# Input projections of the even mixer block as three passes over rounded and remainder parts, in a two-layer diffusion backbone on one core

## What is computed

```python
def half_ffn(h, mod, j, w, g, b, alpha):
    y = swiglu(modulate(h, mod, j), *w)          # (silu(h @ gate) * (h @ up)) @ down
    return layer_norm(alpha * h + 0.5 * gate(mod, j) * y, g, b)
# even layer: h <- LN(a*h + g_1 * W_out[mixers(mod_1(h) @ W_in)])
# W_in columns: NA q, k, v (512 each), mLSTM xm, v, o (512 each), 8 + 8 gate columns
def even_mixer(zc, zl, rpb, conv_w, conv_b, wq, wk, i_bias, f_bias, gn_w):
    pc, pl = split_cols(zc, EV_SIZES), split_cols(zl, EV_SIZES)
    na_c = context_attention(heads(pc[0]), heads(pc[1]), heads(pc[2]))
    na_l = neighbourhood_attention(..., heads(pc[1]), heads(pc[2]), rpb)
    xs_c, o_c = mlstm_prepare(pc[3:], conv_w, conv_b, wq, wk, i_bias, f_bias)
    ...
    h_c, h_l = bidir_scan(mlstm_scan, xs_c, xs_l, ((), ()), init, 2)
```

## Time and profile before

| | us |
|---|---|
| median of 3 runs | 2009.19 (2009.07 to 2010.22) |
| span of the profiled execution | 2008.5 |
| TensorE busy | 1905.3 (95%) |
| VectorE busy | 1263.0 (63%) |
| ScalarE busy | 648.5 (32%) |
| GpSimd busy | 290.2 (14%) |

### The profile page before, as it was taken

One profiled execution on the slowest core, in us unless ns is written; L12 is line 12 of the kernel. 1 busy time (PEld: TensorE's weight loads), 2 busy tenths in 40 slices (PEclk: granted clock), 3 DMA queues, 4 the chain that ended last, 5 costly groups with the idle time before them and its releaser, 6 DMA issues.

```text
span 2008.5 us, 24119 instructions
## 1 busy us (share of the span) xinstructions
PE 1905.3 (95%) x9168; PEld 1512.3 (75%) x9168; DVE 1263.0 (63%) x2217; ACT 648.5 (32%) x1102; POOL 290.2 (14%) x313
## 2 busy tenths in 40 slices
PE   5999999999998789899999989999999899989997
PEld 5888878884554455788887878888778866879997
DVE  7677777664864573877769367673777444464454
ACT  2322242323334441422224233222433232434453
POOL 0000001160000003400001131000044435130002
PEclk7999999999997899899999989999999999989999
DMA  9354545431440001454543233544134644204543
GB/s 363 123 199 182 190 161 153 146 120 61 177 179 0 1 0 43 158 198 175 206 175 144 87 155 132 204 172 177 48 134 176 252 179 152 89 38 168 196 157 108
DMA packets 43958, 290.10 MB, mean 144 GB/s; under 512 B 13916, under 2 KB 19676, under 8 KB 27232
## 3 DMA queue, kind: packets, MB, share of 16 engines
q1 hardware_dynamic: 35488, 271.13, 36.8%
q10 hardware_dynamic: 8384, 17.83, 2.3%
HBM read 272.16 MB, written 16.78 MB: 144 GB/s over the span
## 4 chain that ended last, share of the span: by engine, by line
PE 83%; DVE 9%; DMA 4%; ACT 3%; issue 1%; POOL 0%; SPq 0%; ACTq 0%; POOLq 0%; DVEq 0%
PE bank L623 13%; PE bank L628 13%; PE bank L625 13%; PE bank L680 6%; PE bank L689 6%; PE bank L686 6%; PE bank L810 4%; PE bank L807 3%; PE bank L794 3%; PE bank L989 2%; DMA slot<-in_down_dram 2%; PE bank L747 2%; DMA R<-in_ada_dram 1%; PE bank L737 1%; PE bank L986 1%; PE bank L944 1%
## 5 line engine op out<-in xcount | busy, mean ns | idle before, releaser
L1720 DVE CUSTOM_DVE_ANT_0 L<-slot 128x1024 f32<-128x1024 f32 x272 | 337.6, 1241 | 86.1 <-DMA slot<-in_ada_dram 79.0
L1173 ACT ACTIVATE w_hi<-slot 128x1024 fp32r<-128x1024 f32 x176 | 186.3, 1061 | 572.4 <-PE bank L628 561.2
L1777 DVE TENSOR_TENSOR w_lo<-slot,w_hi 128x1024 fp32r<-128x1024 f32 x176 | 216.8, 1234 | 206.6 <-ACT w_hi L1173 200.4
L623 PE MATMUL bank<-m_hi,w_hi 128*128 128x512 f32 (+1 forms) x1344 | 296.6, 363 | 3.2 <-ACT w_hi L1173 3.2
L628 PE MATMUL bank<-m_hi,w_lo 128*128 128x512 f32 (+1 forms) x1344 | 296.1, 362 | 0.0
L625 PE MATMUL bank<-m_lo,w_hi 128*128 128x512 f32 (+1 forms) x1344 | 296.1, 362 | 0.0
L623 PEld LDWEIGHTS bank<-m_hi,w_hi 128*128 128x128 f32 x1344 | 232.3, 189 | 43.1 <-ACT w_hi L1173 4.0
L628 PEld LDWEIGHTS bank<-m_hi,w_lo 128*128 128x128 f32 x1344 | 232.6, 189 | 39.3
L625 PEld LDWEIGHTS bank<-m_lo,w_hi 128*128 128x128 f32 x1344 | 232.6, 189 | 39.2
L1939 DVE TENSOR_TENSOR down_lo<-slot,down_hi 128x1408 fp32r<-128x1408 f32 x64 | 108.4, 1709 | 127.1 <-ACT down_hi L1223 126.8
L686 PE MATMUL bank<-g_lo,down_hi 128*128 128x512 f32 (+1 forms) x770 | 156.0, 351 | 0.1
(11 more groups left out here) (351 smaller groups left out, 2604.0 us busy)
## 6 DMA issues: line engine op xcount, KB each, us to landing
slot<-in_gateup_dram SPq DMA_DIRECT2D x44, 2048.0 KB, 8.0
slot<-in_ada_dram SPq DMA_DIRECT2D x34, 2048.0 KB, 8.1
slot<-in_down_dram SPq DMA_DIRECT2D x32, 1408.0 KB, 6.2
slot<-in_ev_in_dram SPq DMA_DIRECT2D x4, 2048.0 KB, 8.4
slot<-in_od_in_dram SPq DMA_DIRECT2D x4, 2048.0 KB, 9.2
R<-s_ops SPq DMA_DIRECT2D x16, 512.0 KB, 6.3
s_tables<-slot ACTq DMA_DIRECT2D x8, 768.0 KB, 3.3
R<-s_tables SPq DMA_DIRECT2D x8, 768.0 KB, 7.0
```

The costliest lines, as they stand in the source:

```text
L623: nc.tensor.matmul(bank[j][:, c0:T], w_hi[:, off, c, :], m_hi[:, c, c0:T], start=(c == 0), stop=False)
L1173: nc.scalar.activation(w_hi[:, off, :, :].rearrange("p a b -> p (a b)"), slots[b][:, (2 * (f % 2) + off) * D:(2 * (f % 2) + off + 1) * D], ...
L1720: ins = nc.vector.tensor_tensor_reduce(out=junk, in0=slots[k][:, t * D:(t + 1) * D], in1=csilu[s_], scale=1.0, scalar=0.0, op0=ALU.mult, o ...
L1777: nc.vector.tensor_tensor(w_lo[b][:, t, :, :].rearrange("p a b -> p (a b)"), slots[b][:, t * D:(t + 1) * D], w_hi[:, off, :, :].bitcast(F3 ...
```

## The change

The even block's input projections are made in three passes, as the feed-forwards are. The input is rounded into `even_m_hi` and its remainder kept in `m_lo`. The first slot (xm) is loaded before the third down tile of ffn0, and its four tiles are rounded and subtracted in the down tiles 2 to 5 (`first_tile_hi`, `first_tile_lo`). The other tiles are 21 parts (`PARTS`) that use slots 0 and 1 in turn. ScalarE rounds part u + 2 into one of two buffers (`part_hi`) when part u is done; VectorE subtracts it at the places written out in `even` and `REST_BEFORE`. TensorE makes 24 products for a part. The value slots are now cut by input chunks (`even_values`), so that their four token tiles finish together. The S5 batches stand behind the parts of `OPERATORS_BEHIND`, their transpositions behind those of `TURN_BEHIND`. The bias loads move behind the load of q, the masking of the bias from VectorE to GpSimd, the bias itself to slot 2, NA v to slot 0; so the first half of the output weights is loaded after attention. GpSimd's gains of ffn0 now wait for the last remainder of the input, as they do ahead of a feed-forward.

```diff
@@ -55,9 +55,17 @@
 EXP_MAX = 85.0
 
 
-EVEN_LOADS = [(0, "ev_in", 0, SLOT), (1, "ev_gates", None, KT * 4 * HEADS), (3, "ev_in", 1, SLOT), (2, "ev_in", 2, SLOT),
-              (0, "ev_in", 3, SLOT), (1, "ev_v", 0, SLOT), (2, "ev_v", 1, SLOT), (3, "ml_qk", None, 2 * WIDTH),
-              (0, "ev_out", 0, SLOT), (1, "ev_out", 1, SLOT)]
+EVEN_LOADS = [(0, "ev_in", 0, SLOT), (3, "ev_gates", None, KT * 4 * HEADS), (1, "ev_in", 1, SLOT), (0, "ev_in", 2, SLOT),
+              (1, "ev_in", 3, SLOT), (0, "ev_v", 0, SLOT), (1, "ev_v", 1, SLOT), (3, "ml_qk", None, 2 * WIDTH),
+              (1, "ev_out", 1, SLOT), (0, "ev_out", 0, SLOT)]
+
+
+PARTS = ([("zo", 1, j) for j in range(2)] + [("gates", 3, 0)] + [("zo", 1, j) for j in range(2, 4)] + [("q", 0, j) for j in range(4)]
+         + [("k", 1, j) for j in range(4)] + [("na_v", 0, j) for j in range(4)] + [("ml_v", 1, j) for j in range(4)])
+FIRST_PARTS = 4
+TURN_BEHIND = {4: 0, 5: 1, 8: 2, 10: 3, 12: 4, 13: 5, 15: 6, 17: 7}
+OPERATORS_BEHIND = {7: 0, 9: 1, 11: 2, 12: 3, 14: 4, 16: 5, 17: 6, 19: 7}
+REST_BEFORE = {0: (7,), 1: (8, 9), 2: (10, 11), 3: (12,), 4: (13, 14), 5: (15, 16), 6: (17,), 7: (18, 19)}
 
 
...
+        gate_lo = rounded("gate_lo", slots_at[3], 1024 + KT * 16, [P, KT, P])
+
+        def inputs_of(stage):
+
+            return even_m_hi if stage == "even" else m_hi
         w_lo = [rounded(f"w{b}_lo", slots_at[b], 0, [P, 4, KT, P]) for b in range(2)]
 
...
+                    if d == 2 and s == 0:
+                        load(0, i["ev_in"][0])
+                        loads[0] += 1
...
-                        if n == 1:
+                        if n == 0:
+                            continue
+                        if n == 2:
                             sp.wait_ge(sem("r_ready"), before("r_ready", "ffn0") + KT)
+                        if n == len(EVEN_LOADS) - 1:
+                            sp.wait_ge(sem("even_y0"), 8)
+                        load(k, i[src] if at is None else i[src][at], width=width, at=1024 if src == "ev_gates" else 0)
+                        loads[k] += 1
                         if n == 3:
-                            sp.wait_ge(sem("na_bias_masked"), 8)
-                        load(k, i[src] if at is None else i[src][at], width=width)
-                        loads[k] += 1
+                            bias_loads()
...
+                for s_ in range(2):
+                    a, b = STREAMS[s_]
+                    lo = lambda j, c: nc.tensor.matmul(banks[j][:, a:b], first_hi[:, j, c, :], m_lo[:, c, a:b], start=False, stop=(c == KT - 1))
+                    for c in range(KT):
+                        pe.wait_ge(sem("m_ready"), before_m("even", s_) + c + 1)
+                        for j in range(4):
+                            if s_ == 0 and c == 0:
+                                pe.wait_ge(sem("part_lo_ready"), j + 1)
+                            nc.tensor.matmul(banks[j][:, a:b], first_hi[:, j, c, :], even_m_hi[:, c, a:b], start=(c == 0), stop=False)
+                            nc.tensor.matmul(banks[j][:, a:b], w_lo[0][:, j, c, :], even_m_hi[:, c, a:b], start=False, stop=False)
+                        if c >= late:
+                            pe.wait_ge(sem("m_lo_ready"), before_lo("even", s_) + c - late + 1)
+                            for j in range(4):
+                                lo(j, c - late)
+                    for c in range(KT - late, KT):
+                        pe.wait_ge(sem("m_lo_ready"), before_lo("even", s_) + c + 1)
+                        for j in range(4):
...
+            def even_tile(u, n, bank):
+
+                what, k, j = PARTS[u]
+                w_rest = gate_lo if what == "gates" else w_lo[k][:, j, :, :]
+                if j == 0:
+                    take(k)
+                if n is not None and n >= 4:
+                    pe.wait_ge(sem("even_proj_read"), n - 3)
+                pe.wait_ge(sem("part_hi_ready"), FIRST_PARTS + u + 1)
+                for c in range(KT):
+                    nc.tensor.matmul(bank, part_hi[:, u % 2, c, :], even_m_hi[:, c, :], start=(c == 0), stop=False)
+                for c in range(KT):
+                    nc.tensor.matmul(bank, part_hi[:, u % 2, c, :], m_lo[:, c, :], start=False, stop=False)
+                pe.wait_ge(sem("part_lo_ready"), FIRST_PARTS + u + 1)
+                for c in range(KT):
+                    last = nc.tensor.matmul(bank, w_rest[:, c, :], even_m_hi[:, c, :], start=False, stop=(c == KT - 1))
+                last.then_inc(used[k] if j == 3 or what == "gates" else sem("even_proj_done"), 1)
...
                 for j in range(4):
-                    n = at + j
-                    if n >= 4:
-                        pe.wait_ge(sem(f"{name}_proj_read"), n - 3)
-                    for c in range(KT):
-                        if token_major:
-                            last = nc.tensor.matmul(banks[n % 4][:, :], m[:, c, j * P:(j + 1) * P],
-                                                    slots[k][:, c * WIDTH:(c + 1) * WIDTH], start=(c == 0), stop=(c == KT - 1))
-                        else:
-                            last = nc.tensor.matmul(banks[n % 4][:, c0:T], wslot(k)[:, j, c, :], m[:, c, c0:T],
-                                                    start=(c == 0), stop=(c == KT - 1))
-                    last.then_inc(used[k] if j == 3 else sem(f"{name}_proj_done"), 1)
-                    if behind and j < 2:
-                        behind(j)
-                    if n == 11:
-                        pe.wait_ge(sem("even_rows_ready"), 4)
-                        turn_raw(0)
-                    if 12 <= n < 20:
-                        if n < 19:
-                            turn_raw(n - 11)
-                        s5_operators(n - 12)
+                    if q == 0:
+                        pe.wait_ge(sem("even_proj_read"), n + j - 3)
+                    for c in range(2):
+                        nc.tensor.matmul(banks[j][:, :], tokens(even_m_hi, c, j), hi[:, c, :], start=(q == 0 and c == 0), stop=False)
+                        nc.tensor.matmul(banks[j][:, :], tokens(m_lo, c, j), hi[:, c, :], start=False, stop=False)
+                pe.wait_ge(sem("part_lo_ready"), FIRST_PARTS + u + 1)
+                for j in range(4):
+                    for c in range(2):
+                        last = nc.tensor.matmul(banks[j][:, :], tokens(even_m_hi, c, j), rest_[:, c, :], start=False, stop=(q == 3 and c == 1))
+                    if q == 3:
...
+                first_tiles()
+                n = 4
+                for u, (what, k, j) in enumerate(PARTS):
+                    if what == "gates":
+                        even_tile(u, None, banks[4][:, :])
+                    elif what in ("na_v", "ml_v"):
+                        even_values(u, n)
+                        n += 4 if j == 3 else 0
+                    else:
+                        even_tile(u, n, banks[n % 4][:, :])
+                        n += 1
+                    if u in OPERATORS_BEHIND:
+                        s5_operators(OPERATORS_BEHIND[u])
+                    if u in TURN_BEHIND:
+                        if u == 4:
+                            pe.wait_ge(sem("even_rows_ready"), 4)
+                        turn_raw(TURN_BEHIND[u])
...
+            def first_tile_hi(j):
+
+                if j == 0:
+                    act.wait_ge(used[2], uses_before("even")[2])
+                    act.wait_ge(full[0], 16 * (uses_before("even")[0] + 1))
+                nc.scalar.activation(first_hi[:, j, :, :].rearrange("p a b -> p (a b)"), slots[0][:, j * D:(j + 1) * D], ACT.Copy).then_inc(sem("part_hi_ready"), 1)
...
+                    if name == "ffn0" and 2 <= d < 6:
+                        first_tile_hi(d - 2)
...
+                def next_hi(u):
+
+                    if u + 2 < len(PARTS):
+                        part_hi_of(u + 2)
...
+                def soft_rows():
+
+                    for hd in range(HEADS):
+                        act.wait_ge(sem("even_conv_done"), hd + 1)
+                        nc.scalar.activation(xc[:, hd, :], xc[:, hd, :], ACT.Silu)
+                    act.wait_ge(sem("even_rows_step"), 1)
+                    nc.scalar.activation(rows[:, 6:8, :], rows[:, 6:8, :], ACT.Exp).then_inc(sem("even_soft"), 1)
+                    act.wait_ge(sem("even_soft"), 1)
+                    nc.scalar.activation(rows[:, 6:8, :], rows[:, 6:8, :], ACT.Ln, bias=1.0).then_inc(sem("even_soft"), 1)
...
+                            if what == "ml_v":
+                                local_out(3)
+                                for b in range(2):
+                                    act.wait_ge(sem(f"s5_ops_written{b}"), 32 * (len(BATCHES) // 2))
+                                act.wait_ge(sem("s5_local_written"), 16 * (len(BATCHES) // 2))
+                            for t in range(TT):
+                                projected("even", n, k)
+                                if t == TT - 1:
```

(98 more changed lines are left out.)

176 lines of the change are left out of this document (94 added, 82 removed).

## The result

The changed kernel takes 2012.94 us, the kernel before 2010.12 us in the runs beside it (20 each): a ratio of 1.0015, 95% interval 1.0008 to 1.0021. Forecast were 2000.5 us and faster; it is some 3 us slower, inside what counts as no change. The sign was wrong, the time missed by 12.4 us, and the range (to 2008) did not hold it. Against the kernel before in the runs beside it the miss is 11.5 us (2.8 slower instead of 8.7 faster); the other 0.9 is the distance of that kernel's two medians, 2010.12 and 2009.19.

What follows compares the result with a forecast made beforehand. TensorE was taken to bound the even input projections. They end 15.9 us earlier (3.3 + 30.0 - 0.6 - 11.7 - 5.5 + 0.4); less 3.7 and 2 x 1.75, 8.7 us from 2009.19 gives 2000.5 us, range 1992 to 2008.

Steps and rivals of the forecast that it cites:

- The passes: Even input projections: three passes make each of 21 tiles 5.44 us instead of 6.87, 30.0 us less.
- The first four tiles: Start of the input projections: 192 products of 256 columns end at 444.0 against 447.27, 3.3 us less.
- rival 4: First four tiles run at half clock, costing up to 23.0 us more, 2023.5 us; chance 10%.
- rival 5: Passes not cheaper here: 24 products cost 6.15 us, half of the 30 us gone, 2015.5 us; chance 5%.
- The wait in the second query tile: TensorE stands 11.7 us for part 6's remainder, queued on VectorE behind the gate-row work, which waits for ScalarE's softplus.
- The load ahead of the third down tile: In ffn0, two megabytes ahead of this tile's weights delay them 4.7 us; TensorE stands 3.7 us.
- Rival 1: The load ahead of the third down tile is hidden anyway, costing neither wait nor clock, 1995 us; chance 12%.
- The half clock behind it: Lower clock behind the waits at the third down tile and second query tile: 1.75 us lost for each.
- Even the tile behind the S5 parameter work ... is covered: First down products: that tile wants its first remainder only 5 us in, so 1.2 us more subtraction is covered.
- The tail: End of projections: value reads start 9.4 us after the last batch leaves TensorE, no longer hidden, 5.5 us lost.
- Rivals 2 and 3: VectorE sets the operator batches' pace, 4.3 us, 10%; GpSimd's gains block the first convolution, 1.7 us, 15%.

Runs made afterwards that it cites:

- experiment 5: Changed kernel with only the remainder of part 6 put ahead of VectorE's wait for the logarithm; ratio 1.0011 to the kernel before.
- experiment 6: Changed kernel with Exp and Ln moved right behind the gate rows, remainders of parts 5 and 6 inside VectorE's row work; ratio 0.9980 to the kernel before.
- experiment 3: Changed kernel with the first output-weight load issued only once the last local sum is written; ratio 0.9982 to the kernel before.
- experiment 10: Kernel with all edits together, and the third pass (weight remainder by rounded input) left out of the 21 parts; 1983.38 us, ratio 0.9861 to the kernel before.
- experiment 1: Changed kernel with the first even slot loaded ahead of the fourth down tile's weights, not the third's; 2005.9 us, ratio 0.9978 to the kernel before.
- experiment 7: Changed kernel with Exp and Ln early as in experiment 6, and the eight mask adds moved from GpSimd to VectorE; ratio 0.9946 to the kernel before.

## Why the prediction was wrong

Step by step, with the term as forecast and as measured:

- **The passes, 21 x 1.43 = 30.0 us.** Right: 5.44 us a part. The busy time fell by 29.3 us and not by the 33.3 of these passes and the first tiles together, as the products at half clock behind the two waits took 4.5 us more.
- **The first four tiles, 3.3 us.** Measured from the context statistics (417.27 to 452.29 against 409.35 to 447.27) 2.9 us. Their clock was full (1.00 over 417.27 to 452.73); rival 4 did not occur. Nor did rival 5.
- **The wait in the second query tile, 11.7 us.** Right to the tenth, in its parts too (9.8 us on ScalarE and 11.4 on VectorE against 9.5 of products, as forecast), and right in its mechanism: experiment 5 shows that it is the chain softplus, row work, S5 batch, experiment 6 that it goes when the chain starts earlier.
- **The load ahead of the third down tile, 3.7 us.** Measured 4.0, with the weights 15.5 us from issue to landing instead of 11.0. Rival 1 did not occur. The half clock behind it was 2.5 instead of 1.75 us, and behind the query tile 2.0. "Even the tile behind the S5 parameter work ... is covered" was off by 0.5 us. In all the context statistics came 7.9 us later, 0.4 of it drift from before 311 us, where 5.45 was forecast.
- **The tail, 5.5 us.** This is the step that failed most. From the last batch's end on TensorE (602.70) to the reads (616.69) it took 14.0 us, not the 9.4 of the earlier trace rows. I had taken 9.4 us as the length of the tail and not asked what else would be on its way. Before, the last output weights, issued at 584.43, landed 8.1 us later and so some 1.4 us ahead of the write at 593.96: the 9.4 us were themselves only just free of such a neighbour. The change frees slot 1 exactly when the last product ends, and SP fills it at once. The write took 5.7 us more, the steps ahead of it 1.2 us less: the price is 4.6 us, and experiment 3, with a tail of 8.2 us, gives back more than that.
- **A term that was missing: the S5 read, 3.4 us.** The same mistake. The order of the slots was changed, so the second value slot is now requested as the last k tile ends, some 3 us ahead of ScalarE's request for the raw matrices of batch 5. I had counted the loads' own cover and not who stands beside them.
- **Rivals 2 and 3.** VectorE did not set the pace, but experiment 10 shows how near it is. GpSimd's gains ended at 452.38, just before the convolution began (452.67), and its four two-input steps took 3.10 us as in the kernel before. The one-input step that opens a head was stretched beside GpSimd's fills and copy, to 0.89 and 1.30 us in the first two heads instead of 0.54; TensorE, busy all through, did not wait for it.

Against the forecast the attention start is 12.3 us late: 0.4 drift, 2.0 the down tile, 0.4 the first tiles, 3.4 the S5 read, 0.2 clock behind the query tile, 4.6 the tail; 11.0 together. The other 1.3 us are spread over the parts: behind each of the eight S5 batches the first eight products of a part take 1.91 to 1.93 us instead of 1.81, and before some of them stands 0.2 us. That these 1.3 us lie there is read from the chain alone; no experiment tests it. The forecast's range left out what a neighbouring 2 MB transfer does to a small one on the path. With it (3.4 and 4.6 us) the sum gives some 2008.5 us, within 0.2% of no change.

## What to carry to other kernels

- When loads change their order, write down for each small transfer on the path which large one is issued in the microseconds ahead of it, from any queue. A load whose slot comes free early can be held back by one wait that costs nothing: here two such waits and one load moved by a tile were worth 16 us.
- A saving on the bounding engine is only had where the engines behind it keep up: go along the slack of each (VectorE here had 8 us for 30), and expect a wait to come back at the next link if only its named link is moved.
- A wait of TensorE can cost more than itself: behind those of 4 and 12 us the products lost 2 to 2.5 us at half clock, behind the one of 3.4 us nothing in the changed kernel's profile, while in the profiles of experiments 1, 6 and 7 the granted clock over the 5 us behind that same wait was 0.50, 0.66 and 0.66.

## What the runs showed of the hardware

- A 256 KB write took 8.09 us with a 2 MB load issued 0.16 us ahead of it on another queue, and 2.35 us without; a 128 KB read 8.4 instead of 2.7 us. The Trainium skill (DMA: Bandwidth & Descriptors, section "Queues, rings and completion order") says that each DMA engine serves its queues in turn, a packet at a time. If both transfers have as many packets to an engine, the small one would end with the large one, which is what is seen. The profile counts 144 packets for the load from 608 to 617 us and 211 on ScalarE's queue (the write, and the end of an operator write ahead of it), so the small one has not fewer. This fits but was not tested; whether the small transfer itself moved slowly or was only reported late is open too.
- GpSimd's mask adds (two SBUF inputs, 1.3 to 3.4 us each in experiment 6) and VectorE's two-input instructions slow each other: 2.20, 2.35, 2.21, 2.30 and 1.70 us against 1.21, 1.21, 1.23, 1.21 and 0.65. Either side can be the one that stretches: a subtraction took its usual 1.21 us while the add around it took 3.40. GpSimd's fills, which only write, left the two-input steps of the convolution at 3.10 us for four. The Trainium skill (SBUF — State Buffer, section "Who interferes with whom") states both for instructions with two SBUF inputs, a conflict with an instruction that reads and none with one that only writes, and the trace agrees. A one-input step is another case: in the changed kernel one took 1.30 us beside a fill instead of 0.54.
